# Rotary embedding in a fused two-block kernel: TensorE's ten products with a rotation matrix become ScalarE copies between partitions

## What is computed

```python
def rope(t, pos):
    half = t.shape[-1] // 2
    inv = ROPE_THETA ** (-jnp.arange(half, dtype=jnp.float32) / half)
    ang = pos.astype(jnp.float32)[..., None] * inv
    cos = jnp.cos(ang)[:, :, None, :]
    sin = jnp.sin(ang)[:, :, None, :]
    t1 = t[..., :half].astype(jnp.float32)
    t2 = t[..., half:].astype(jnp.float32)
    return jnp.concatenate([t1 * cos - t2 * sin, t2 * cos + t1 * sin], axis=-1).astype(t.dtype)

        z = u @ w_in[i]
        (aq, ak, av, iq, ik, iw, rq, rk, rv, rg, ga, gb) = jnp.split(z, split_points, axis=-1)
        aq = rope(aq.reshape(b, s, A_HEADS, A_HEAD_DIM), positions)
        ak = rope(ak[:, :, None, :], positions)[:, :, 0, :]
        iq = rope(iq.reshape(b, s, IDX_HEADS, IDX_DIM), positions) * (IDX_DIM ** -0.5)
        ik = rope(ik[:, :, None, :], positions)[:, :, 0, :]
        y_a = dsa_attention(aq, ak, av, iq, ik, iw, n_sel)
        rq = rope(rq.reshape(b, s, R_HEADS, R_QK_DIM), positions).astype(jnp.float32)
        rk = rope(rk.reshape(b, s, R_HEADS, R_QK_DIM), positions).astype(jnp.float32)
```

## Time and profile before

| | us |
|---|---|
| runs | 1196.19, 1200.89, 1200.97; median 1200.89 |
| the profiled execution | 1196.29 |
| its span | 1194.2 |
| PE busy | 1117.0 (94%) |
| DVE busy | 712.5 (60%) |
| ACT busy | 496.2 (42%) |
| the mixer's part with the ten embeddings | 684 to 803 after the span's start |

### The profile page before, as it was taken

The page is one execution under the profiler, slowest core; times in us unless marked ns, Lnnn a source line. Parts: engine busy times, 40 slices in busy tenths (PEclk is TensorE's granted clock), DMA queues, the critical chain, the costliest instruction groups (busy, mean ns, idle before and its releaser), DMA issues.

```text
span 1194.2 us, 19109 instructions
## 1 busy us (share of the span) xinstructions
PE 1117.0 (94%) x8002; PEld 951.1 (80%) x8002; DVE 712.5 (60%) x1124; ACT 496.2 (42%) x751; POOL 0.2 (0%) x4
## 2 busy tenths in 40 slices
PE   5899988899999998799999999999999999999985
PEld 3688867555555555799999887997889999999985
DVE  1879777322223326867565686977645775655576
ACT  3674223111111113644344544338954563444353
POOL 0000000000000000000000000000000000000000
PEclk9899997899999999899999999999999999999998
DMA  9945617999999955364544433323236545454410
GB/s 384 377 166 221 244 42 309 411 422 413 401 413 404 398 218 206 108 272 151 207 179 168 167 106 107 132 107 113 100 142 221 177 177 212 177 181 172 156 57 36
DMA packets 38153, 258.38 MB, mean 216 GB/s; under 512 B 4368, under 2 KB 5136, under 8 KB 7856
## 3 DMA queue, kind: packets, MB, share of 16 engines
q1 hardware_dynamic: 36720, 252.90, 55.1%
q10 hardware_dynamic: 1344, 4.21, 0.9%
HBM read 256.05 MB, written 1.05 MB: 215 GB/s over the span
## 4 chain that ended last, share of the span: by engine, by line
PE 73%; DVE 8%; ACT 3%; issue 1%; DVEq 0%; ACTq 0%
PE bank L515 72%; DVE wl L1702 1%; ACT wh L1192 1%; DVE acc L1764 1%; DVE xt L1752 1%; DVE rstd L1726 1%; DVE hl L1769 1%; PE bank L890 0%; ACT L1202 0%; PE bank L848 0%; DVE arena L1920 0%; DVE xt L2175 0%; DVE xt L2463 0%; ACT arena L1566 0%; DVE yl L1722 0%
## 5 line engine op out<-in xcount | busy, mean ns | idle before, releaser
L515 PE MATMUL bank<-hh,wh 128*128 128x256 f32 (+1 forms) x1256 | 367.4, 293 | 8.3 <-DVE hl L1722 3.8
L515 PE MATMUL bank<-hl,wh 128*128 128x256 f32 (+1 forms) x1256 | 361.7, 288 | 0.0
L515 PE MATMUL bank<-hh,wl 128*128 128x256 f32 (+1 forms) x1256 | 361.6, 288 | 0.0
L1702 DVE TENSOR_TENSOR wl<-raw,wh 128x1024 fp32r<-128x1024 f32 (+2 forms) x236 | 267.0, 1168 | 95.5 <-ACT wh L1192 94.2
L1192 ACT ACTIVATE wh<-raw 128x1024 fp32r<-128x1024 f32 (+2 forms) x236 | 227.1, 1006 | 78.9 <-PE bank L515 77.7
L515 PEld LDWEIGHTS bank<-hh,wh 128*128 128x128 f32 x1256 | 244.3, 194 | 16.4 <-issue 10.3
L515 PEld LDWEIGHTS bank<-hl,wh 128*128 128x128 f32 x1256 | 244.3, 195 | 1.9 <-issue 0.5
L515 PEld LDWEIGHTS bank<-hh,wl 128*128 128x128 f32 x1256 | 244.1, 194 | 1.2
L515 PE MATMUL bank<-yh,wh 128*128 128x256 f32 x512 | 148.6, 290 | 8.3 <-DVE yl L1722 6.7
L515 PE MATMUL bank<-yl,wh 128*128 128x256 f32 x512 | 147.0, 287 | 0.0
L515 PE MATMUL bank<-yh,wl 128*128 128x256 f32 x512 | 146.8, 287 | 0.0
(11 more groups left out here) (243 smaller groups left out, 1351.8 us busy)
## 6 DMA issues: line engine op xcount, KB each, us to landing
raw<-in_gu SPq DMA_DIRECT2D x40, 1024.0 KB, 11.0
arena<-in_gu SPq DMA_DIRECT2D x24, 1024.0 KB, 9.7
raw<-in_gd SPq DMA_DIRECT2D x22, 1024.0 KB, 8.6
raw<-in_w_adt SPq DMA_DIRECT2D x14, 1024.0 KB, 6.1
raw<-in_f1g SPq DMA_DIRECT2D x11, 1024.0 KB, 4.9
raw<-in_f2g SPq DMA_DIRECT2D x11, 1024.0 KB, 4.8
raw<-in_f2u SPq DMA_DIRECT2D x11, 1024.0 KB, 4.9
raw<-in_f2d SPq DMA_DIRECT2D x11, 1024.0 KB, 4.8
```

The lines of the kernel that those rows point to most:

```text
L515: return pe.matmul(o, l, m, start=start, stop=stop, skip_group_check=True)
L1702: v.tensor_tensor(WL[slot_of[U]][:, 0:n], src, WH[slot_of[U]][:, 0:n].bitcast(f32), ALU.subtract).then_inc(S("wl"), 1)
```

## The change

PE's ten products go, with their two constant matrices (half of what the first load of constants brings) and their banks. In their place ACT copies blocks of 32 or 64 partitions of `TR` to the partitions half a head away, in the buffer `TA` (`shifted`): four instructions for a piece with heads of 64, two for one with heads of 128. The minus sign of the first half moves to the table of sines: the factor of the angle is negative for these partitions. Since there is one `TA`, `shifted(x)` first waits until embedding x - 1 is finished. It stands directly behind the copy of the piece in ACT's list; for x = 0 and 1, which DVE brings, it stands behind the eight copies of the norm and behind the weight splits of ik.

```diff
-CON = [("ident", 128), ("sel", 4), ("ones", 128), ("ra", 128), ("rr", 128), ("inv", 2), ("idxw", 8), ("scanm", 512),
+CON = [("ident", 128), ("sel", 4), ("ones", 128), ("inv", 2), ("idxw", 8), ("scanm", 512),
...
-            def rotate(x, name, T, n, kind):
-                b = take(pe, ("rot", x))
-                evicted(pe, name)
-                mm(b[:, 0:n * 256], cst("rr" if kind else "ra"), T[:, 0:n, :].rearrange("p k t -> p (k t)"), True, True).then_inc(S("rot"), 1)
-
...
                 copy_out(name, T[:, 0:n, :], two(bank(name))[:, 0:n, :])
+                evicted(a, name)
+                shifted(x, T, n, 3 <= x < 7)
+
+            def shifted(x, T, n, kind):
+                if x:
+                    a.wait_ge(*nth("rope", x))
+                half = 64 if kind else 32
+                for p in range(0, 128, half):
+                    q = p + half if p // half % 2 == 0 else p - half
+                    t = a.activation(TA[p:p + half, 0:n, :], T[q:q + half, 0:n, :], ACT.Copy)
+                t.then_inc(S("rot"), 1)
...
+            evicted(a, ("iq", 0))
+            shifted(0, TR[0], 2, 0)
             ahead("w2iq", 1)
             ahead("w2ik", 0)
+            evicted(a, ("iq", 1))
+            shifted(1, TR[1], 2, 0)
             rope_in(2, "ik", ("w2ik", 0), TR[0], 1)
...
                 v.wait_ge(*nth("rot", x + 1))
-                v.tensor_tensor(T, two(bank(("rot", x)))[:, 0:n, :], s, ALU.mult).then_inc(copied(("rot", x)), 1)
-                evicted(v, ("rot", x))
+                step(v.tensor_tensor(T, TA[:, 0:n, :], s, ALU.mult))
+                prev()
...
-        inv[:, c] = t[np.arange(128) % half]
+        inv[:, c] = t[np.arange(128) % half] * np.where(np.arange(128) // half % 2, f(1), f(-1))
```

More of the change, by code:

```diff
@@ L441, in program @@
         job("q_stat", 3)
-        put(("iq", 0), ("iq", 1), ("rot", 0), "ik", "ikw", ("rot", 1))
+        put(("iq", 0), ("iq", 1), "ik", "ikw")
         ix_jobs = lambda *n: put(*[("ix", k) for k in n])
-        put(("rq", 0), ("rot", 2))
+        put(("rq", 0))
         ix_jobs(0, 1)
-        put(("rq", 1), ("rot", 3))
+        put(("rq", 1))
         ix_jobs(2, 3, 4, 5)
-        put(("rk", 0), ("rot", 4))
+        put(("rk", 0))
         ix_jobs(6, 7)
-        put(("rk", 1), ("rot", 5))
-        put(("rv", 0), ("rot", 6))
+        put(("rk", 1))
+        put(("rv", 0))
         put(("rv", 1), ("rs", 0))
@@ L455, in program @@
         put(("aq", 0), ("rvar", 0), ("rm", 1), ("rw", 2), ("rs", 3))
-        put(("aq", 1), ("rot", 7), ("rvar", 1), ("rm", 2), ("rw", 3))
-        put("ak", "av", ("rot", 8), ("rvar", 2), ("rm", 3), ("rot", 9))
+        put(("aq", 1), ("rvar", 1), ("rm", 2), ("rw", 3))
+        put("ak", "av", ("rvar", 2), ("rm", 3))
         at_jobs = lambda n: put(*([("atv", (n - 3) // 2)] if n >= 3 and n % 2 else []),
@@ L1096, in tensor_program @@
             lin_fm(("w2iq", 1), [take(pe, ("iq", 1))], H0, L0)
-            rotate(0, ("iq", 0), TR[0], 2, 0)
             lin_mixed(("w2ik", 0), take(pe, "ik"), take(pe, "ikw"), 8, H1, L1, hn)
-            rotate(1, ("iq", 1), TR[1], 2, 0)
             lin_fm(("w2rq", 0), [take(pe, ("rq", 0))], H1, L1)
-            rotate(2, "ik", TR[0], 1, 0)
             logits_ix(0, 2)
             lin_fm(("w2rq", 1), [take(pe, ("rq", 1))], H1, L1)
-            rotate(3, ("rq", 0), TR[1], 2, 1)
             logits_ix(2, 6)
             lin_fm(("w2rk", 0), [take(pe, ("rk", 0))], H1, L1)
-            rotate(4, ("rq", 1), TR[0], 2, 1)
             logits_ix(6, 8)
             lin_fm(("w2rk", 1), [take(pe, ("rk", 1))], H1, L1)
-            rotate(5, ("rk", 0), TR[1], 2, 1)
             lin_tm(("w2rv", 0), [take(pe, ("rv", 0))], 2, H1, L1)
-            rotate(6, ("rk", 1), TR[0], 2, 1)
             lin_tm(("w2rv", 1), [take(pe, ("rv", 1))], 2, H1, L1)
@@ L1127, in tensor_program @@
             lin_fm(("w2aq", 1), [take(pe, ("aq", 1))], H1, L1)
-            rotate(7, ("aq", 0), TR[1], 2, 0)
             ret_var(1)
@@ L1132, in tensor_program @@
             lin_mixed(("w2kv", 0), take(pe, "ak"), take(pe, "av"), 64, H1, L1)
-            rotate(8, ("aq", 1), TR[0], 2, 0)
             ret_var(2)
             ret_mean(3)
-            rotate(9, "ak", TR[1], 1, 0)
             for h in range(4):
@@ L2513, in constants @@
     parts["ones"] = np.ones((128, 128), f)
[L2514 to L2522, removed]
     inv = np.zeros((128, 2), f)
```

## The result

| | before | after |
|---|---|---|
| median of 16 runs each, us | 1196.43 | 1206.13 |
| lowest and highest, us | 1193.29, 1201.39 | 1201.85, 1211.05 |
| ratio, 95% interval | | 1.0082 (1.0069 to 1.0094) |
| span of the profiled execution, us | 1194.2 | 1208.5 |
| PE, DVE, ACT busy, us | 1117.0, 712.5, 496.2 | 1124.2, 712.5, 514.3 |

What follows compares the result with a forecast made beforehand. The prediction took the DVE and ACT chain up to attention step 0 as the bound: 3.7 us delay, plus 0.3 clock, minus 0.3 loading, is 3.7 us slower; on the median of 1200.89 this gives 1204.6 us, range 1197 to 1209.5.

Steps and rivals of the forecast that it cites:

- the sum: Whole kernel: chain delay 3.7, clock 0.3, smaller constant load -0.3, so 3.7 us slower; with near neighbours, chance 0.57.
- The likelier class: Whole kernel: time the same within 0.5% (6.0 us), chance 0.58.
- slower, at 0.36: Whole kernel: slower by over 0.5%, chance 0.36.
- What bounds the kernel: Between 684 and 803 us: the DVE and ACT chain up to attention step 0 decides, not PE's 7.7 us less work.
- The price of a copy: ACT's copies: 0.50 us per 512-column piece, 0.60 at most; a set of four 2.0 us (1.44 to 2.4).
- Third place: Heads 0 to 3, sets 7 to 9: reciprocals late by 2.25, 4.4, 4.2 and 3.7 us; sets the end.
- First place: Embeddings 0 to 2: embedding 2 ends 2.4 us late, PE idles 5 us or more ahead of the index products.
- The clock at the index products: Behind PE's wait for embedding 2: granted clock falls to 0.50, costing 1.5 us.
- Second place: The search, behind rk 1 and embedding 6: starts 0.4 us late and carries this to 772.
- 3 x 0.85: PE from 713 until rk 1 ends: time given back by rotations gone, leaving PE 2.2 us late instead of 3.9.
- The clock rival: Clock falls at index products, head 3's squares and attention steps 0, 1, 2: 7.9 us slower, 1208.8; chance 0.35.
- The bounds of 1.61 (no) and 2.33 (yes): PE's waits: clock stays at 1.00 behind 1.61 us, falls behind 2.33; about 2 us at step 0 taken to fall.

Runs made afterwards that it cites:

- e1: The changed kernel with PE making ten products of the old size at the old places again, result unused; 1208.65 us, 1.0082 to the kernel before.
- e3: The changed kernel with each set of two or four copies made one copy of 128 partitions, without the rotation; 1196.11 us, 0.9978 to before.
- e9: The changed kernel with two buffers, some weight splits moved ahead of sets 0 and 2, and sets 7 to 9 directly behind the roots; 1192.16 us, 0.9962.
- e8: The changed kernel, one buffer, only ACT's order changed: splits ahead of sets 0 and 2, sets 7 to 9 behind the squares; 1200.40 us, 1.0023.
- e4: The changed kernel with a second buffer for the rotated rows, so set x waits for embedding x - 2; 1199.72 us, 1.0011 to before.
- e2: The changed kernel with the pieces copied to their own partitions, without the rotation; 1205.32 us, 1.0057 to before.
- e5: The changed kernel with x = 7, 8 and 9 rotated by PE again, ACT's copies kept for 0 to 6; 1200.44 us, 1.0026 to before.
- e7: The changed kernel with ACT's copies only for x = 3 to 6 and the six others rotated by PE; 1192.91 us, 0.9965 to before.
- e12: e9 with two unused spare products on PE ahead of the first index products; 1188.70 us, 0.9925 to before.
- e10: e9 with x = 0 rotated by PE again; 1189.29 us, 0.9928 to before.
- e6: The changed kernel with x = 0, 1 and 2 rotated by PE again, ACT's copies kept for 3 to 9; 1201.25 us, 1.0026 to before.
- e11: The changed kernel with eight unused spare products on PE ahead of the first index products; 1205.28 us, 1.0057 to before.

## Why the prediction was right, and where it was not

The forecast 1204.6 and its range held the measured 1206.13. Part of that is luck: it counted from 1200.89, the median of three runs, and before's median of 16 is 1196.43. Of the effect itself +3.7 was forecast and +9.8 measured: the sum was 6.1 us short. The likelier class, within 0.5%, did not come; slower, at 0.36, did.

- **What bounds the kernel: right.** The chain between DVE and ACT sets the reciprocals, and PE's 7.7 us do not show in the runs (e1).
- **The price of a copy: too low, and past its bound.** I took 0.50 a piece with 0.60 as the most; it is 0.64, since pieces of 0.627 us do not overlap at all. The Trainium skill (ScalarE: Activation LUTs, What ACT_TABLE_LOAD costs) gives an overlap of about 93 ns between neighbours. The full-width copy of e3 shows it (691.15 + 0.42 - 691.48 = 0.09), the pieces of 32 and 64 partitions do not. A set was 2.55 instead of 2.0.
- **Third place: right in form.** Forecast growths from the search on, at the four heads: 1.85 (2.25 less the search's 0.4), 2.15, -0.2, -0.5. Measured, as differences along after's row: 2.4, 2.7, 0.1, -0.6. The buffer's wait at sets 8 and 9 is there (3.11).
- **First place: embedding 2 was forecast 2.4 late and was 3.35.** Two sets of four that are 0.55 longer stand ahead of it, about this difference. PE's wait was 8.08 us, where the forecast's terms make 5.6: PE reached it 3.7 us earlier than before, not 2.1, the cost of the three products that are gone by then. In before the granted clock was 0.50 from about 702 to 706, with PE busy, and in after's profile it was not:

```profile
702.00:704.00 2.00, 2.00 (x12) 2.00 (x11) 1.97 (x4) 1.50 (x2) 0.00 (x0) 0.55 0.21 29
704.00:706.00 2.00, 2.00 (x13) 2.00 (x13) 1.97 (x4) 0.00 (x0) 0.00 (x0) 0.60 0.81 315
```

- **The clock at the index products: the term that failed.** I priced it at 1.5 us, from 16 products of 128x256 behind the wait of 2.33. It took 3.6 to 3.7. Here the granted clock was 0.50 from before the first product to about 727, 8.5 us behind the wait's end, while in before 1.00 came back within 5 us of the wait's end at 684.29, as the row behind the earlier trace rows shows:

```profile
688.00:690.00 2.00, 2.00 (x16) 2.00 (x16) 1.88 (x5) 0.97 (x3) 0.00 (x0) 0.87 0.00 0
```

  I took one loss behind one wait as the loss behind any. The length of the wait does not order the losses at this place: by the same stretch, less 8.12, they were 2.8 us behind waits of 2.98, 2.99 and 6.61 (e9, e8, e4), 3.1 behind 5.54 (e3), 3.6 behind 4.43 (e1, less the spare product in the stretch) and 3.6 to 3.7 behind 7.92 to 8.08 (e2, e5, after). What the products behind the wait do to it was not tried.
- **Second place: the step that failed most.** I had the search 0.4 late; it was 4.96, about 4.6 of the 6.1 us that the sum was short. (The "3 x 0.85" given back until rk 1 ends is a slip: 2.2 follows from two products.) PE reaches rk 1 5.3 late instead of 2.2 (748.37 - 688.76 against 738.63 - 684.29): the clock's 2.2 and embedding 2's 1.0 above their forecasts. Set 6 then waited 1.18 us for embedding 5's buffer, a wait I had not counted:

```profile
748.37 0.60 ACT L1187 ACTIVATE arena<-bank 128x512 f32<-128x512 f32 x1 [2.47 <-PE bank L515]
750.14 1.27 ACT L1514 ACTIVATE arena<-arena 64x512 f32<-64x512 f32 x2 [1.18 <-DVE arena L2251]
```

  That 5 us then stood under the third place.
- **The clock rival was nearest,** +7.9, but at the wrong place. I put its losses at the attention steps. One of them came: the clock fell at the squares of head 3 (a wait of 2.91 us), PE came late to step 0, and its transpose started without a wait, 10.2 late where the reciprocal was 9.6:

```profile
816.93 2.05 PE L515 MATMUL bank<-sq,csts 128*128 128x256 f32 x4 [2.91 <-ACT sq L1536]
...
829.28 0.60 PE L1067 MATMUL bank<-csts,arena 128*128 128x128 f32 x4
```

  So the wait of about 2 us that I forecast there, and named as a sign of being right, was not to be seen. The large loss lay at the index products, where my sum had it already, too small.
- **The bounds of 1.61 (no) and 2.33 (yes) for a fall of the clock: not a threshold.** The same wait of 1.61 us at step 0 left it at 1.00 in before, e5, e7 and e12, and in e9 and e10 it fell about 1.2 us behind the wait's end. Waits of 1.54 to 1.57 us at the squares of head 2 in after, e2, e6 and e11 were followed by a fall, too; PE's next wait, for the squares of head 3, takes that loss up. Two stretches behind this wait, first of e10 (transpose at 806.18), then of e12 (at 801.62):

```profile
808.00:810.00 2.00, 2.00 (x8) 1.37 (x7) 1.21 (x2) 1.23 (x3) 0.00 (x0) 0.50 0.09 20
```

```profile
804.00:806.00 2.00, 2.00 (x19) 2.00 (x18) 0.84 (x2) 1.24 (x3) 0.00 (x0) 1.00 0.38 90
```

By the profiles of after, e11 and e7 the delay of 10.2 divides so: 3.6 us for the clock at the index products, 1.3 for embedding 2's own delay as it reaches the search (3.35 less the 2.0 that the middle pieces give back, as in e7), 5.1 for sets 7 and 8 (2.4 and 2.7); heads 2 and 3 and step 0 add 0.1.

## What to carry to other kernels

Work moved to an idle engine costs what its place costs: ask for each moved instruction which short result stands behind it in the engine's list, and put it where that engine waits anyway. The same ten sets of copies made this kernel 0.8% slower in one order and 0.4% faster in another with a second buffer. When PE is left to wait by a faster list, look at the granted clock behind the wait: it can be cheaper to leave PE a product. And compare profiles of two kernels from a common point just ahead of the change.

## What the runs showed of the hardware that I had not expected

- A copy on ACT of 32 or 64 partitions by 512 columns takes 0.627 us, as one of 128 partitions does (0.629), but starts 0.64 behind its forerunner, where the full one lets the next start after 0.52. Moving to other partitions changes nothing (e2).
- Two spare products (1.88 us) in a wait of 2.98 us made the kernel 3.5 us faster (e12 against e9), since the clock stayed at 1.00. Behind waits of 1.05 us the granted clock stayed at 1.00, behind 1.54, 2.31, 2.91, 2.98, 5.54 and 8.08 it was 0.50, and 1.61 us went both ways. It also fell with PE busy and no wait just ahead: for about 3.4 us from 702 in before, for about 10 us from 697 in e6.
- Two executions of the same instructions differ by several us: the anchor lay at 688.76 in after and at 678.08 in e12, which are the same ahead of it, with a mean granted clock of 0.95 and 0.97 up to there.
- Behind the wait of 8.08 us 1.2 GHz lasted 8.5 us more in after, though PE was busy for most of them.
